# Order of weight roundings and PSUM banks in the two hybrid mixers of a two-block network

## Chip, cores and metric

The kernel runs on one core of a Trainium2 chip. The metric is the device time of one execution in microseconds, from the first to the last instruction of the core with what lies around it. The names of the engines in profile rows: PE is TensorE (PEld its weight loads), DVE is VectorE, ACT is ScalarE, POOL is GpSimd, SP is the engine that issues most of the DMAs.

## What is computed

The program is a whole network on a sequence of 512 tokens with 1024 features. The first block has two layers; each is half a feed-forward network, a hybrid mixer, and half a feed-forward network again. The second block (a bidirectional delta-rule mixer, experts) isn't touched. Of the reference, cut to the mixer:

```python
def first_block(x, ...):
    for l in range(2):
        x = x + 0.5 * swiglu_ffn(rms_norm(x, ffn1_norm_w[l]), ...)
        x = x + hybrid_mixer(rms_norm(x, mix_norm_w[l]), l, w_in[l], w_out[l], ...)
        x = x + 0.5 * swiglu_ffn(rms_norm(x, ffn2_norm_w[l]), ...)

def hybrid_mixer(h, ...):
    proj = h @ w_in
    mq, mk, mv, mo, mi, mf, z, xbc, dt_raw, dq, dk, dv = split(proj)
    # mLSTM of mq, mk, mv with the gates mi, mf; norm; times sigmoid(mo)
    xbc = silu(causal_dwconv(xbc, conv_w, conv_b))
    # state-space scan of xbc with dt_raw; times silu(z); norm
    # differential attention: two softmaxes of dq, dk with a bias,
    # first minus lam times second, times dv; norm
    return concatenate([y_mlstm, y_ssm, y_diff]) @ w_out
```

## The kernel before

Every engine has its own instruction stream, and each stage is a Python class that writes all of them. The class `Mixer` is the hybrid mixer; it is built twice, for layer 0 (it begins at about 434 us of the trace) and for layer 1 (at about 1634 us). `steps()` yields pairs (name, number), and `pe`, `act`, `dve` and `pool` walk over the same list of steps, each writing its own engine's share of a step. So the list sets the order on every engine, and a step that an engine has no share in costs it nothing.

**Weights.** Float32 precision comes from three products of rounded parts: a weight unit is 128x1024, and its high part (a cast to the rounded type on ScalarE, line 388) and its low part (weight minus high part, line 167) are made on the chip; `mm3` multiplies high by high, high by low and low by high. The step "split" j does both for unit j. The low part is made by VectorE for the mixer's units 0 to 3 and by GpSimd for all others (`lower`). There are three places for rounded units, so unit j may be cast only when the projection that read unit j-3 is done. `ahead(i)` yields "split" i+2.

**Projections.** `items` lists the mixer's 26 half blocks of `w_in`, numbered 0 to 25: xbc 0 to 7, mq and mk 8 to 11, mv 12 and 13, dq and dk 14 to 17, dv 18 and 19, z 20 to 23, mo 24 and 25, and then w_out. Item i reads unit i. The kind "fm" makes 128 output features for all tokens (24 products 128x512, a bank of its own for each of two in turn, `bank`). The kind "tok" makes 256 features for two token tiles at a time, and each of its two items needs both units of the pair: 12 products with the first unit, then 12 with the second, for each tile (`tok_pe`). The step "sum" i is item i on TensorE; "suma" i is the first half of an item (one token tile for "tok") which `steps` places before the left-over steps of the item before. Items 0 to 2 multiply the raw input (`raw_pe`), since the norm isn't there yet; VectorE multiplies their results by the norm's factor when it reads them (`raw_read`, within `scale_dve`, after inputs 1, 4 and 7). Item 3 and all later ones read the scaled input, of which `scale_dve` makes eight pieces (L177 and L167 in turn, with a cast on ScalarE, L494, between).

**Start of a mixer.** Steps: split 2, item 0, norm, split 3, item 1, scale, split 4, item 2 and so on. "norm" is on TensorE four sums over features, on VectorE mean and reciprocal (L173, L476), on TensorE the spread of the reciprocals (within item 1, behind its first two inputs), on ScalarE a table load and the square root. Item 2 waits until `there(0)`, VectorE's read of item 0, since both use bank 4. Behind item 5 TensorE transposes the small gate projections (line 157, 32x16); it waits for VectorE's copy L536, which stands in VectorE's order behind the convolutions of xbc.

**Attention.** "diff" n, n from 0 to 18, is a pipeline over 16 tiles (4 heads with 4 query tiles). On TensorE: the product with the values of tile n-3, the logits of tile n, the transposes of tile n-2. On ScalarE: a copy of the values' product (L2013), a copy of the transposes (L2018), and last the two exponentials of tile n (L182), which wait for VectorE. On VectorE: normalising tile n-1, adding scale and bias to the logits of tile n (L177, from PSUM), the maximum (L2052) and its negation (L172, 128x2). The steps of a projection are followed by those of `behind(i)`, of which `CUT` tells how many come before the next item's first half; for items 21 and 23 that is "diff" 3, "diff" 4 and "diff" 9, "diff" 10. For the second item of a "tok" pair, `ahead` follows the item's "sum": split 23 before "diff" 3, split 25 before "diff" 9.

Of the kernel before, what the change touches and what calls it, by code (L numbers as in the profile page):

```python
# [322 lines left out]
class Dense(Stage):  # L323
# [130 lines left out]
    def norm_pe(self, e, bank, n, there):  # L454

        self.norm_sum(e, bank, n, there)
        self.norm_spread(e, bank, n)
# [363 lines left out]
class Delta(Stage):  # L821
# [30 lines left out]
    def steps(self):  # L852
        for name in self.SETUP[4:] if self.ready else self.SETUP:
            yield name, 0
        for r in range(len(self.rounds)):
            for n in self.NAMES:
                yield n, r
                for x in self.after.during(r, n) if self.after else ():
                    yield ("then", *x), r
# [309 lines left out]
class Context(Conv):  # L1169
# [37 lines left out]
    def bank(self, i):  # L1207
        return self.k.bank[4 + i % 2]
# [324 lines left out]
class Mixer(Dense):  # L1533
# [125 lines left out]

    CUT = {6: 0, 7: 0, 13: 2, 14: 1, 15: 1, 16: 2, 17: 2, 18: 1, 21: 2, 22: 2, 23: 2, 24: 3}  # L1660

    def behind(self, i):

        if i == 0:
            yield "norm", 0
        elif i == 1:
            yield "scale", 0
        elif i == 3:
            yield "small", 0
        elif i == 4:  # L1670
            yield "ones", 0
        elif i == 5:
            yield "gates", 0
        elif i == 6:
            yield "cum", 0
        elif i == 7:
            yield "xs", 0
            yield "bias", 0
        elif i == 8:
            yield "silu", 7  # L1680
        for which, h in self.SSM.get(i, ()):
            yield "s" + which, h
        if i == 13:
            yield "crow", 0
        elif i == 14:
            yield "mt", 0
            yield "mA", 0
        if 16 <= i <= 19:
            yield "dsum", i - 16
        if 15 <= i <= 17:  # L1690
            yield "mA", i - 14
        if 15 <= i <= 18:
            yield "mB", i - 15
        if i == 19:
            yield "droot", 0
            for j in range(5):
                yield "mnorm", j
            yield "mroot", 0
        elif i == 20:
            for j in (0, 2, 1, 3):  # L1700
                yield "dfin", j
            yield "diff", 0
            yield "diff", 1
        elif 20 < i < 25:
            yield "diff", 3 * (i - 21) + 3
            if i == 24:
                yield "ssq", 1
            yield "diff", 3 * (i - 21) + 4
            yield "mnorm", i - 16
            if i == 24:  # L1710
                yield "sroot", 0
            yield "diff", 3 * (i - 21) + 5
        if i in (21, 23):
            yield "zgate", i // 2 - 10
        elif i == 22:
            yield "ssq", 0
        elif i == 24:
            yield "snorm", 0

    def steps(self):  # L1720
        yield "zero", 0
        yield from self.first()
        left = []
        for i in range(self.np):
            late = self.items[i].kind == "tok" and self.items[i].half
            if not late:
                yield from self.ahead(i)
            if left or i > 20:
                yield "suma", i
                yield from left  # L1730
                if i == 21:
                    yield "diff", 2
            yield "sum", i
            if late:
                yield from self.ahead(i)
            todo = list(self.behind(i))
            n = self.CUT.get(i, len(todo))
            yield from todo[:n]
            left = todo[n:]
        yield "diff", 15  # L1740
        yield "turn", 2
        yield "turn", 3
        yield "mo", 0
        yield "diff", 16
        yield "parts", 2
        yield "parts", 3
        yield "turn", 0
        yield "turn", 1
        yield "snorm", 1
        yield "diff", 17  # L1750
        yield "dnorm", 0
        yield "dnorm", 1
        yield "parts", 0
        yield "parts", 1
        yield "turn", 4
        yield "turn", 5
        yield "diff", 18
        yield "dnorm", 2
        yield "dnorm", 3
        yield "parts", 4  # L1760
        yield "parts", 5
        yield "part", 0
        yield "part", 1
        for t in range(5):
            yield "dnorm", 4 + t
        for c in (6, 7):
            yield "turn", c
            yield "parts", c
        for i in range(self.np, len(self.items)):
            yield from self.ahead(i)  # L1770
            yield "sum", i
# [14 lines left out]
    def bank(self, i):  # L1786

        if i >= self.np:
            return 4 + (i - self.np) % 4
        return 4 + self.nth(i) % 2  # L1790

    def nth(self, i):
        return sum(it.kind == "fm" for it in self.items[:i])
# [17 lines left out]
    def pe(self, e):  # L1811
        k, P, S, V, K, B = self.k, self.P, self.S, self.V, self.k.K, self.k.bank
        for name, i in self.steps():
# [7 lines left out]
                self.norm_spread(e, B[7], 512)  # L1821
                self.raw_pe(e, 1, range(2, 8))
            elif name == "sum" and i == 2:
                e.wait_ge(self.there(0))
                self.raw_pe(e, 2, range(8))
            elif name in ("sum", "suma") and i < self.np:
                it = self.items[i]
# [1687 lines left out]
```

## Time and profile before

| | |
|---|---|
| median of 3 runs | 3306.43 us (3302.94 to 3307.87) |
| the profiled execution | 3301.13 us, span 3299.3 us |
| PE busy | 3083.2 us (93%), x17336 |
| DVE busy | 1653.5 us (50%) |
| ACT busy | 1052.1 us (32%) |
| POOL busy | 217.6 us (7%) |
| granted TensorE clock, mean | 0.966 |

The profile is one execution. A busy share is an average over stages with different limits; what a change in a stage is worth is read from that stage's waits. In a timeline row the first number is the start, the second the duration, and the bracket at the end tells how long the engine stood idle before it and what released it.

### The profile page before, as it was taken

How to read it: one execution, taken by the hardware profiler on the slowest of the kernel's cores; microseconds unless marked ns; L12 is line 12 of the kernel's file. 1: busy time of each engine (PE TensorE's matmuls, PEld its weight loads, DVE VectorE, ACT ScalarE, POOL GpSimd, SP SyncE). 2: the span in 40 equal slices, each digit the busy share in tenths (PEclk: the TensorE clock that was granted, in tenths of full speed). 3: DMA queues.
4: the chain of work that ended last, by engine and by line, in shares of the span. 5: the costliest groups of instructions: out<-in, count | busy, mean ns of one | idle time of the engine just before them, and what ended most of it. 6: DMA issues, size and time to landing. Idle time of an engine off the chain costs nothing. (4 is left out here: it accounts for less than half of the span.)

```text
span 3299.3 us, 42166 instructions
## 1 busy us (share of the span) xinstructions
PE 3083.2 (93%) x17336; PEld 2349.0 (71%) x17336; DVE 1653.5 (50%) x3143; ACT 1052.1 (32%) x2148; POOL 217.6 (7%) x165
## 2 busy tenths in 40 slices
PE   8999999979999999999999889999898998887887
PEld 6777778768888878888778778888687887333333
DVE  5444485375555564555674564444644675211212
ACT  4222244353323243333344342222342553000002
POOL 0000012121000000000022220000001110000000
PEclk9999999989999999999999899999899889899999
DMA  4444421102223222122211112222211004999997
GB/s 187 185 163 150 150 84 61 42 27 96 96 77 124 81 96 93 68 71 83 90 52 52 39 52 92 92 92 90 86 64 64 2 2 195 366 420 421 421 421 328
DMA packets 66168, 443.39 MB, mean 134 GB/s; under 512 B 7476, under 2 KB 7732, under 8 KB 19640
## 3 DMA queue, kind: packets, MB, share of 16 engines
q1 hardware_dynamic: 61632, 425.75, 33.6%
q10 hardware_dynamic: 2648, 8.39, 0.7%
q0 software_dynamic: 1696, 6.55, 0.5%
q8 instruction: 137, 2.24, 0.3%
q14 instruction: 55, 0.45, 0.0%
HBM read 435.16 MB, written 5.51 MB: 134 GB/s over the span
## 5 line engine op out<-in xcount | busy, mean ns | idle before, releaser
L157 PE MATMUL ps<-b,b 128*128 128x512 f32 (+6 forms) x14038 | 2795.1, 391 | 153.1 <-DVE b L167 48.4
L157 PEld LDWEIGHTS ps<-b,b 128*128 128x128 f32 (+3 forms) x14038 | 2091.3, 183 | 821.7 <-issue 311.6
L167 DVE TENSOR_TENSOR b<-b,b 128x1024 fp32r<-128x1024 f32 (+7 forms) x743 | 611.8, 828 | 286.4 <-ACT b L388 167.0
L388 ACT CAST b<-b 128x1024 fp32r<-128x1024 f32 (+2 forms) x408 | 391.6, 961 | 419.8 <-PE ps L157 412.9
L167 DVE TENSOR_TENSOR b<-ps,b 128x64 f32<-128x64 f32 (+5 forms) x626 | 219.7, 366 | 299.3 <-PE ps L157 247.7
L157 PE MATMUL ps<-b 64*64 64x64 f32 (+10 forms) x2848 | 248.9, 276 | 31.2 <-ACT b L2018 17.4
L167 POOL TENSOR_TENSOR b<-b,b 128x1024 fp32r<-128x1024 f32 (+3 forms) x112 | 183.0, 1651 | 1368.1 <-ACT b L388 937.9
L157 PEld LDWEIGHTS ps<-b 64*64 64x64 f32 (+3 forms) x2848 | 211.6, 159 | 64.2 <-issue 20.2
L177 DVE SCALAR_TENSOR_TENSOR b<-ps,b 128x512 f32<-128x512 f32 (+3 forms) x272 | 142.4, 545 | 210.2 <-PE ps L157 184.6
L183 ACT ACTIVATE b<-b 128x512 f32<-128x512 f32 (+7 forms) x287 | 151.2, 533 | 210.8 <-DVE b L177 169.6
L167 DVE TENSOR_TENSOR b<-b,ps 128x512 f32<-128x512 f32 (+1 forms) x114 | 77.1, 678 | 279.5 <-PE ps L157 276.8
L177 DVE SCALAR_TENSOR_TENSOR b<-b,b,b 128x512 f32<-128x512 f32 (+3 forms) x224 | 170.4, 773 | 48.0 <-ACT b L183 43.7
L177 DVE SCALAR_TENSOR_TENSOR b<-ps,b,b 128x128 f32<-128x128 f32 (+3 forms) x164 | 83.5, 536 | 214.3 <-ACT b L183 116.7
L1479 ACT CAST b<-b 128x512 fp32r<-128x512 f32 x88 | 54.6, 621 | 412.7 <-DVE b L167 412.7
L183 ACT ACTIVATE b<-ps 128x512 f32<-128x512 f32 (+5 forms) x114 | 48.3, 437 | 338.7 <-PE ps L157 337.7
L177 DVE SCALAR_TENSOR_TENSOR b<-b,b 128x512 f32<-128x512 f32 (+6 forms) x235 | 135.0, 589 | 41.3 <-ACT b L183 39.0
L183 ACT ACTIVATE b<-b,b 128x128 f32<-128x128 f32 (+2 forms) x252 | 110.6, 477 | 140.4 <-DVE b L167 97.1
L183 ACT ACTIVATE b<-ps,b 128x128 f32<-128x128 f32 (+3 forms) x142 | 55.8, 432 | 122.9 <-PE ps L157 121.8
L286 PE MATMUL ps<-b,b 128*128 128x128 f32 (+1 forms) x450 | 73.5, 302 | 20.5 <-DVE b L177 9.4
L286 PEld LDWEIGHTS ps<-b,b 128*128 128x128 f32 (+1 forms) x450 | 54.6, 153 | 52.6 <-issue 25.0
L1044 ACT COPY b<-ps 128x128 f32<-128x128 f32 x240 | 60.2, 269 | 80.1 <-PE ps L157 71.0
L1159 POOL MEMSET b<- 128x128 f32 x12 | 2.5, 258 | 1005.0 <-DVE b L2695 581.5
(106 smaller groups left out, 569.0 us busy)
## 6 DMA issues: line engine op xcount, KB each, us to landing
b<-in_eg SPq DMA_DIRECT2D x64, 1024.0 KB, 27.4
b<-in_eu SPq DMA_DIRECT2D x64, 1024.0 KB, 27.2
b<-in_ed SPq DMA_DIRECT2D x64, 1024.0 KB, 26.9
b<-in_wg SPq DMA_DIRECT2D x44, 1024.0 KB, 4.8
b<-in_wu SPq DMA_DIRECT2D x44, 1024.0 KB, 4.8
b<-in_win SPq DMA_DIRECT2D x40, 1024.0 KB, 4.8
b<-in_wd SPq DMA_DIRECT2D x48, 768.0 KB, 4.1
b<-in_wmod SPq DMA_DIRECT2D x24, 1024.0 KB, 4.8
```

Of the source, the lines that this page charges most:

```text
L157: return e.h.matmul(out, l, r, start=start, stop=stop)
L167: return e.h.tensor_tensor(out, a, b, op)
L177: return e.h.scalar_tensor_tensor(out, a, s, b, op0, op1)
L183: return e.h.activation(out, a, f, bias=bias, scale=scale)
L286: return e.h.transpose(out, i, self.K["ident"][0:n, 0:n])
L388: e.h.copy(hi, src).then_inc(*self.S.tick(("hi", i)))
L1044: e.h.copy(self.LB[q][:, 0:128], B[:, 0:128]).then_inc(*S.tick((s, j, "L", lev + 1)))
L1159: z = e.h.memset(t, 0.0)
L1479: e.h.copy(self.ahi[:, f - self.f0[grp], :], t).then_inc(*S.tick(("ahi", f)))
```

## The change

In `behind(0)` the step "split" 3 is put ahead of "norm" (and left out ahead of item 1). Items 2 and 3 get the banks 0 and 1, which nobody else uses at that time; item 2's wait for `there(0)` goes, and with it, through `bank`, item 3's wait for the read of item 1, while items 4 and 5 wait for the reads of items 0 and 1 and not of 2 and 3. For items 21 and 23 the "split" moves behind the first step of `behind(i)` (`SPLIT`): "diff" 3, split 23, "diff" 4, and "diff" 9, split 25, "diff" 10. For the other second items of pairs the order stays.

```diff
--- before.py
+++ after.py
@@ -1659,9 +1659,12 @@
 
     CUT = {6: 0, 7: 0, 13: 2, 14: 1, 15: 1, 16: 2, 17: 2, 18: 1, 21: 2, 22: 2, 23: 2, 24: 3}
 
+    SPLIT = {21: 1, 23: 1}
+
     def behind(self, i):
 
         if i == 0:
+            yield from self.ahead(1)
             yield "norm", 0
         elif i == 1:
             yield "scale", 0
@@ -1723,7 +1726,7 @@
         left = []
         for i in range(self.np):
             late = self.items[i].kind == "tok" and self.items[i].half
-            if not late:
+            if not late and i != 1:
                 yield from self.ahead(i)
             if left or i > 20:
                 yield "suma", i
@@ -1731,10 +1734,11 @@
                 if i == 21:
                     yield "diff", 2
             yield "sum", i
-            if late:
-                yield from self.ahead(i)
             todo = list(self.behind(i))
             n = self.CUT.get(i, len(todo))
+            if late:
+                todo[self.SPLIT.get(i, 0):0] = self.ahead(i)
+                n += 1
             yield from todo[:n]
             left = todo[n:]
         yield "diff", 15
@@ -1787,7 +1791,7 @@
 
         if i >= self.np:
             return 4 + (i - self.np) % 4
-        return 4 + self.nth(i) % 2
+        return i - 2 if 2 <= i < 4 else 4 + self.nth(i) % 2
 
     def nth(self, i):
         return sum(it.kind == "fm" for it in self.items[:i])
@@ -1821,7 +1825,6 @@
                 self.norm_spread(e, B[7], 512)
                 self.raw_pe(e, 1, range(2, 8))
             elif name == "sum" and i == 2:
-                e.wait_ge(self.there(0))
                 self.raw_pe(e, 2, range(8))
             elif name in ("sum", "suma") and i < self.np:
                 it = self.items[i]
```

ScalarE at the start of the first mixer: the casts to b_125 and b_126 are the high parts of units 2 and 3; the table load, a one-element activation and the square root from PSUM (b_62) are the norm.

```order
 L183 ACTIVATE b_70<-b_60 128x512
 L388 CAST b_125<-b_53 128x1024
+L388 CAST b_126<-b_53 128x1024
 L183 ACT_TABLE_LOAD
 L183 ACTIVATE b_72<-b_72 128x1
 L183 ACTIVATE b_62<-ps 128x512
-L388 CAST b_126<-b_53 128x1024
 L494 CAST b_131<-b_69 128x512
 L494 CAST b_131<-b_70 128x512
```

The cast of unit 3 moved ahead of the norm, and the casts of the scaled inputs follow the square root directly.

VectorE at the same place: b_128 and b_129 are the low parts of units 2 and 3, b_71 the mean and its reciprocal, b_69 and b_70 the first scaled inputs.

```order
 L167 TENSOR_TENSOR b_128<-b_53,b_125 128x1024
+L167 TENSOR_TENSOR b_129<-b_53,b_126 128x1024
 L173 TENSOR_SCALAR b_71<-ps 128x4
 L476 RECIPROCAL b_71<-b_71 128x4
-L167 TENSOR_TENSOR b_129<-b_53,b_126 128x1024
 L177 SCALAR_TENSOR_TENSOR b_69<-b_60,b_56,b_62 128x512
 L177 SCALAR_TENSOR_TENSOR b_70<-b_60,b_56,b_62 128x512
```

The low part of unit 3 stands ahead of the mean and the reciprocal now, and no longer between them and the scaling.

ScalarE behind item 21 in the first mixer, before the change: L183 reads item 21's result, the cast to b_125 is unit 23, L2013 and L2018 are the copies of "diff" 3 and L182 its exponentials; the last two rows are the copies of "diff" 4.

```order
L183 ACTIVATE b_124<-ps 128x2x256
L388 CAST b_125<-b_51 128x1024
L2013 COPY b_124<-ps 128x64
L2018 COPY b_124<-ps 128x256
L182 ACTIVATE b_124,b_118<-b_124,b_118 128x512 x2
L2013 COPY b_124<-ps 128x64
L2018 COPY b_124<-ps 128x384
```

The same place with the change (the line numbers of the copies are three higher):

```order
L183 ACTIVATE b_124<-ps 128x2x256
L2016 COPY b_124<-ps 128x64
L2021 COPY b_124<-ps 128x256
L182 ACTIVATE b_124,b_118<-b_124,b_118 128x512 x2
L388 CAST b_125<-b_51 128x1024
L2016 COPY b_124<-ps 128x64
L2021 COPY b_124<-ps 128x384
```

The cast moved behind the exponentials of tile 3. Unit 25 moves in the same way behind the exponentials of tile 9, and both do so in the second mixer too.

## Rows read from the trace of the kernel before

**Rows 1.** Timeline, all engines, start of the first mixer (start us, us, engine, line; idle before).
```profile
435.61 1.05 ACT L388 CAST b<-b 128x1024 fp32r<-128x1024 f32 x1 [0.90 <-DVE b L167]
...
436.69 1.23 DVE L167 TENSOR_TENSOR b<-b,b 128x1024 fp32r<-128x1024 f32 x1 [0.96 <-ACT b L388]
...
438.02 0.18 DVE L476 RECIPROCAL b<-b 128x4 f32<-128x4 f32 x1
...
440.75 0.60 ACT L183 ACTIVATE b<-ps 128x512 f32<-128x512 f32 x1 [2.58 <-PE ps L157]
...
443.46 1.41 DVE L177 SCALAR_TENSOR_TENSOR b<-b,b,b 128x512 f32<-128x512 f32 x2
...
447.63 0.79 PE L157 MATMUL ps<-b,b 128*128 128x512 f32 x1 [2.72 <-DVE b L167]
```

**Rows 2.** Windows of TensorE: us, busy (count), granted clock, DMA share, GB/s.
```profile
447.50:451.00 3.50, 3.37 (x8) 0.51 0.03 12
```

**Rows 3.** Windows of all engines: PE, PEld, DVE, ACT, POOL busy, then clock.
```profile
441.60:485.50 43.90, 40.19 (x168) 30.78 (x167) 42.15 (x52) 15.54 (x22) 9.86 (x4) 0.92 0.20 72
```

**Rows 4.** Timeline of PE, first mixer, the join behind the sixth projection.
```profile
476.30 12.03 PE L157 MATMUL ps<-b,b 32*128 32x16 f32 x52 [0.99 <-DVE b L536]
```

**Rows 5.** Timeline of DVE, ACT and PE, the same places of the second mixer.
```profile
1638.62 0.18 DVE L476 RECIPROCAL b<-b 128x4 f32<-128x4 f32 x1
...
1642.76 1.41 DVE L177 SCALAR_TENSOR_TENSOR b<-b,b,b 128x512 f32<-128x512 f32 x2
...
1640.05 0.60 ACT L183 ACTIVATE b<-ps 128x512 f32<-128x512 f32 x1 [1.27 <-PE ps L157]
...
1646.93 26.13 PE L157 MATMUL ps<-b,b 128*128 128x512 f32 x112 [2.75 <-DVE b L167]
1675.61 14.62 PE L157 MATMUL ps<-b,b 32*128 32x16 f32 x62 [2.54 <-DVE b L536]
```

**Rows 6.** Timeline, all engines, attention tiles 3 to 5 of the first mixer.
```profile
652.59 1.03 ACT L388 CAST b<-b 128x1024 fp32r<-128x1024 f32 x1
...
653.69 2.36 POOL L167 TENSOR_TENSOR b<-b,b 128x1024 fp32r<-128x1024 f32 x1 [13.35 <-ACT b L388]
654.05 1.38 PE L157 MATMUL ps<-b 128*128 128x64 f32 x8 [2.51 <-ACT b L2018]
...
655.67 4.61 PE L157 MATMUL ps<-b,b 128*128 128x256 f32 x24
...
657.04 0.71 ACT L182 ACTIVATE b<-b,b 128x512 f32<-128x512 f32 x1
...
660.11 1.41 PE L157 MATMUL ps<-b 128*128 128x64 f32 x10
...
660.37 0.17 DVE L172 TENSOR_SCALAR b<-b 128x2 f32<-128x2 f32 x1
...
662.47 2.40 POOL L167 TENSOR_TENSOR b<-b,b 128x1024 fp32r<-128x1024 f32 x1 [6.41 <-ACT b L388]
662.47 0.75 DVE L177 SCALAR_TENSOR_TENSOR b<-ps,b 128x256 f32<-128x256 f32 x2
...
663.91 0.98 DVE L172 TENSOR_SCALAR b<-b 128x2 f32<-128x2 f32 x1
```

**Rows 7.** Timeline, all engines, attention tiles 9 and 10 of the first mixer.
```profile
685.96 0.17 DVE L172 TENSOR_SCALAR b<-b 128x2 f32<-128x2 f32 x1
...
687.00 0.51 ACT L182 ACTIVATE b<-b,b 128x256 f32<-128x256 f32 x1
...
687.16 3.55 PE L157 MATMUL ps<-b 128*128 128x64 f32 x12 [3.05 <-ACT b L2018]
...
690.74 1.02 DVE L177 SCALAR_TENSOR_TENSOR b<-ps,b 128x384 f32<-128x384 f32 x2 [0.87 <-PE ps L157]
```

**Rows 8.** Timeline of the second mixer, attention tile 9.
```profile
1884.97 0.17 DVE L172 TENSOR_SCALAR b<-b 128x2 f32<-128x2 f32 x1
...
1885.77 0.51 ACT L182 ACTIVATE b<-b,b 128x256 f32<-128x256 f32 x1
```

## Prediction

> **What bounds the kernel now.** TensorE is busy for 93% of the span, so I looked for the places where it stands still and asked what ended each wait. The change touches only the two mixers, and in each only three places: the start, attention tile 3 and attention tile 9. I read the timeline of all engines there, then windows for the granted clock, and left the rest of the program alone.
>
> At the start of the first mixer TensorE waits 2.72 us before projection 2, for the VectorE read of projection 0 that empties bank 4 [rows 1]. In the second mixer it is 2.75 us [rows 5]. Behind the first of these waits the granted clock was 0.51 for 3.50 us, the 1.2 GHz level [rows 2]; that costs about 1.7 us of TensorE work. But VectorE is the engine to watch: from the rounding of projection 3's weights onwards it is busy 42.15 of 43.90 us [rows 3], and TensorE then waits for it again before the small transposes, 0.99 us in the first mixer [rows 4] and 2.54 us in the second [rows 5]. So the start is a VectorE chain. Its head is: reciprocal of the norm, spread on TensorE, square root on ScalarE, the rounding of unit 3, and then the first scale at 443.46 [rows 1].
>
> In the attention part the chain goes back and forth between VectorE (logits, maximum, negation, L172) and ScalarE (exponentials, L182). TensorE waits 2.51 us for a copy on ScalarE that stands behind the cast of unit 23 [rows 6], and 3.05 us in the same way at tile 9 [rows 7].
>
> **The change, part by part.** Nothing is added or taken away on any engine; TensorE, GpSimd and the DMA queue keep their order. Three things move.
>
> *A. Start of a mixer.* Unit 3 is cast directly behind unit 2's cast, which ends at 436.66 [rows 1]. A cast lasts 1.03 to 1.05 us, so it is done at 437.7, before VectorE has finished unit 2's low part (436.69 + 1.23 = 437.9). VectorE then does unit 3's low part, 1.15 us of spacing (1.23 less the overlap of neighbours), ahead of mean and reciprocal. The reciprocal ends at 439.35 and not 438.20. Does the square root come 1.15 us later? In the second mixer reciprocal to square root is 1.25 us (1638.80 to 1640.05) [rows 5], so there the whole 1.15 is paid. In the first it is 2.55 us [rows 1]: TensorE was itself late by 1.3, so between 0 and 1.15 is paid, and I take 0.5, since the spread at the lower clock also needs longer than at the higher. The scale follows the square root directly now. First mixer: 441.35 + 0.5 = 441.9 with the hand-over, against 443.46, a gain of 1.5. Second: 1640.65 + 1.15 = 1641.85, against 1642.76, a gain of 0.9. Bounds: 1.0 to 2.0 and 0.3 to 0.9 (the low one if the longer wait for the reciprocal lowers the clock there as in [rows 2]).
>
> The banks: TensorE begins projection 2 without the 2.72 and 2.75 us waits, less the late spread, so 2.2 and 1.6 us sooner, and in the first mixer perhaps without the spell of [rows 2]. I cost this at nothing beyond VectorE's gain, because it ends at the same join: TensorE arrives at the small transposes sooner and waits longer there for VectorE, which has no gap to close [rows 3]. Projections 3 to 5 have their inputs in time, since VectorE's whole chain comes sooner too. **A: -2.4 us.**
>
> *B. Tile 3 (unit 23).* The cast moves from 652.59 behind tile 3's exponentials, and these wait for VectorE; the last ends at 657.75 [rows 6]. So the cast runs 657.75 to 658.8, and GpSimd's low part (start 0.07 behind the cast, 2.36 us long [rows 6]) ends at 661.2 and not 656.05. What wins: the copy before TensorE's 2.51 us wait comes 1.0 sooner. That buys nothing, as the next logits are not read before VectorE's own work is done. What loses: TensorE's next half projection, 24 products [rows 6], takes its last 12 from unit 23. It would reach them at about 656.2 (653.1 for the copy, 1.6 to the first product as now, 1.4 for 12) and must stand until 661.2. Then come 12 products of 256 columns (112 of 512 columns took 26.13 us [rows 5], 0.23 each, so half of that each: 1.4 us) and the block with tile 5's logits, 1.41 [rows 6]: 664.1 with a hand-over. VectorE now reads them at 662.47; it would be 1.7 late. Some of that is given back: tile 5's negation, 0.17 us elsewhere, lasts 0.98 to 664.89, when GpSimd's operation of 662.47 + 2.40 ends [rows 6]; being later it isn't held, so about 0.8 returns. Left: 0.9 us. With one spell at 1.2 GHz after so long a stand it is 1.7 more, 2.6 us. Waits of 2.5 us and more in these rows were followed by one (the 24 products behind the 2.51 us wait took 4.61), so I take 2.6 per mixer; without a spell it is 0.9, with two in a row 4.3. **B: +5.2 us.**
>
> The new low part also lies over tile 4's negation (660.37 [rows 6]), which then ends at 661.2, 0.8 late; this is covered by TensorE's delay above. The Trainium skill ("SBUF — State Buffer", "Who interferes with whom") says that GpSimd and such a VectorE instruction exclude each other for the whole instruction and that issue order decides; the trace agrees, the 0.98 us above end with GpSimd's operation. By that rule the negation could lose a whole GpSimd operation, up to 2.4 us and not 0.8, if it came just behind its start; the sum would be up to 3.2 us more over both mixers.
>
> *C. Tile 9 (unit 25).* The same move, but here the negation was ready at 686.13 and the exponential began only at 687.00 [rows 7], for cast and copies were ahead of it. Without the cast it begins at 686.2: 0.8 gained, and TensorE's logits of tile 10, for which VectorE waited 0.87 us, come sooner by as much. In the second mixer it is 1885.14 against 1885.77 [rows 8], 0.6. Unit 25 is needed later than it is ready here: its cast would follow the second exponential at about 687.2, its low part ends near 690.6, and the products that want it come around 691. Bounds: 0 (if they do wait) to 2.0 and 1.0 (if the shorter wait also avoids the slow spell in the 3.55 us block [rows 7]). **C: -1.4 us.**
>
> DMA: two loads of output weights start behind these low parts, 5.2 and 1.6 us later. They are cast only after the whole attention part, tens of us on: nothing.
>
> **Sum:** -2.4 + 5.2 - 1.4 = +1.4 us. The profiled execution would go from 3301.13 to 3302.5. It lies 5.3 us under the median of the runs, so I apply the difference to the median: 3307.8. A measurement of this kernel tells about 0.2%, 6.6 us, from no change; the forecast is therefore "no difference that can be seen".
>
> **The rivals.**
> 1. *TensorE, not VectorE, sets the start.* Then 2.2 + 1.6 us and the spell's 1.7 count, -5.5 for A; with B at 0.9 twice and C at -1.4 it is -5.1: 3301.3. For it: both bank waits are real and vanish. Against it: [rows 3] leave VectorE under 2 us of slack, and the waits of [rows 4, 5] name it.
> 2. *Late unit 23 costs two spells* (the slower side). TensorE stands almost 5 us in the middle of a half projection, longer than any wait in these rows. With two spells B is 4.3 twice; unit 25's products wait as well and eat C's gain. -2.4 + 8.6 = +6.2: 3312.6. It decides against the change from B over 1.9 us per mixer, and visibly from about 5. Against it: the spell in [rows 2] lasted 3.5 us and ended while TensorE worked on.
> 3. *The start brings nothing.* The change doesn't do there what it says: projection 3 waits for the scaled inputs instead of the bank, and the late reciprocal takes back what the missing cast gave. Then +5.2 - 1.4 = +3.8: 3310.2. Against it: TensorE is not what the chain waits for after the square root.
>
> **How the numbers follow.** Forecast 0.58, rival 1 0.15, rival 2 0.15, rival 3 0.12. The best ends of all parts give -2.9 + 1.8 - 3.0 = -4.1, the worst -1.3 + 8.6 + 0 = +7.3; runs of one kernel here lie up to 3.5 us from their median. The range 3301.5 to 3312.0 takes in the forecast, rival 3, nearly all of the better side and most of rival 2. Over 0.2% faster needs rival 1 with more than its price: 0.05. Over 0.2% slower is the upper part of rival 2: 0.10. The rest, 0.85, is no difference.
>
> **What would show each step.** A: no TensorE wait before projection 2, first scale 1.5 and 0.9 us sooner after the end of the stage before, and a longer wait before the small transposes (about 2 and 3 us). A shorter wait there makes A wrong. B: TensorE stands near 5 us inside the 24 products behind tile 4's logits, with GpSimd as releaser, and the logits of tile 5 come 1.7 to 3.4 us later, counted from tile 3. If the 24 products stay at 3 to 4.6 us without a wait, B is wrong. C: tile 9's exponential directly behind its negation. A whole time outside the range would mean that shifts of a few us change waits or the clock in stages that I left out.

## The result and the profile after

| | before | after |
|---|---|---|
| median | 3303.34 us (3299.1 to 3308.33, 20 runs) | 3309.2 us (3306.48 to 3314.19, 20 runs) |
| ratio, 95% interval | | 1.0019 (1.0012 to 1.0026) |
| profiled execution | 3301.13 us | 3314.19 us, the slowest of its 20 |
| span | 3299.3 us | 3312.3 us |
| mean granted clock | 0.966 | 0.963 |

The change costs about 6 us: a little less than the 0.2% that I called the bound of what can be told, while the interval reaches beyond it. The 20 runs of the kernel before have a median 3.1 us under that of the three runs from which I predicted. One execution of the kernel before, beside the third group of the experiments below, took 7656 us and is in no ratio.

The page of the changed kernel, the span and the busy times:

```profile
span 3312.3 us, 42162 instructions
...
PE 3094.4 (93%) x17336; PEld 2359.9 (71%) x17336; DVE 1652.9 (50%) x3143; ACT 1052.0 (32%) x2148; POOL 219.0 (7%) x165
```

The same instructions are there, but TensorE is busy for 11.2 us more and the span is 13.0 us longer. Work that is the same in number took longer, and the mean granted clock is 0.963 instead of 0.966. (The span's difference is twice that of the medians, since one profile is the slowest of its kernel and the other among the faster ones.) Measured between the same instructions (VectorE's first one of a mixer, a memset, and the reduction of its last norm), the two mixers took 592.2 us before and 601.2 after; everything outside them took 2707.1 and 2711.1, and between 2707.9 and 2711.7 in the profiles of all the experiments. So 9.0 of the 13.0 us are inside the mixers, and the other 4.0 are about what executions differ by anyway.

By stretches, both mixers together, the 9.0 us are: -3.2 from the start to the gate projections, +2.2 from there to attention tile 0, +7.7 from tile 3 to tile 6, +0.2 from tile 9 to tile 11, +1.6 behind the last tile, +0.5 elsewhere. The +2.2 lie in a stretch that the change doesn't touch: in the 28 mixers of all the profiles it took 158.8 to 163.6 us, 161.0 in the mean of the 16 with unit 3 split early and 160.5 in that of the 12 without. How much of a gain at the start is left at tile 0 can't be told against that.

**The start.** Timeline of the changed kernel, all engines, start of the first mixer (start us, duration, engine, line; the bracket is idle time and releaser), which answers to [rows 1]:

```profile
435.89 2.00 ACT L388 CAST b<-b 128x1024 fp32r<-128x1024 f32 x2 [0.90 <-DVE b L167]
...
436.97 2.36 DVE L167 TENSOR_TENSOR b<-b,b 128x1024 fp32r<-128x1024 f32 x2 [0.96 <-ACT b L388]
...
439.44 0.18 DVE L476 RECIPROCAL b<-b 128x4 f32<-128x4 f32 x1
...
440.87 0.60 ACT L183 ACTIVATE b<-ps 128x512 f32<-128x512 f32 x1 [1.46 <-PE ps L157]
...
441.50 1.42 DVE L177 SCALAR_TENSOR_TENSOR b<-b,b,b 128x512 f32<-128x512 f32 x2 [1.88 <-ACT b L183]
```

The two casts and the two low parts stand together now, and the first scale follows the square root directly: 441.50 instead of 443.46, in a mixer that begins 0.28 us later (unit 2's cast at 435.89, not 435.61). Counted from that cast the reciprocal is 1.1 us later, as foreseen, but the square root isn't later at all.

Timeline of PE in the changed kernel, the projections and the join, first mixer and then second, answering to [rows 1, 4, 5]:

```profile
439.67 31.17 PE L157 MATMUL ps<-b,b 128*128 128x128 f32 x138 [1.12 <-DVE b L476]
...
474.36 23.09 PE L157 MATMUL ps<-b,b 32*128 32x16 f32 x100 [3.52 <-DVE b L536]
...
1645.85 31.21 PE L157 MATMUL ps<-b,b 128*128 128x128 f32 x138 [1.14 <-DVE b L476]
1680.54 19.81 PE L157 MATMUL ps<-b,b 32*128 32x16 f32 x91 [3.48 <-DVE b L536]
```

The waits of 2.72 and 2.75 us before projection 2 are gone; the waits at the join grew from 0.99 and 2.54 us to 3.52 and 3.48. TensorE is early and VectorE sets the time of the join.

**Attention tiles 3 to 5.** Timeline of the changed kernel, all engines, answering to [rows 6]:

```profile
653.98 0.38 ACT L2021 COPY b<-ps 128x256 f32<-128x256 f32 x1
654.41 2.64 PE L157 MATMUL ps<-b 128*128 128x64 f32 x8 [1.57 <-ACT b L2021]
...
657.53 2.91 PE L157 MATMUL ps<-b,b 128*128 128x256 f32 x12
...
659.05 1.03 ACT L388 CAST b<-b 128x1024 fp32r<-128x1024 f32 x1
...
660.10 0.75 DVE L177 SCALAR_TENSOR_TENSOR b<-b,b 128x512 f32<-128x512 f32 x1
660.16 2.89 POOL L167 TENSOR_TENSOR b<-b,b 128x1024 fp32r<-128x1024 f32 x1 [20.07 <-ACT b L388]
...
661.67 1.41 DVE L172 TENSOR_SCALAR b<-b 128x2 f32<-128x2 f32 x1
...
663.10 2.93 PE L157 MATMUL ps<-b,b 128*128 128x256 f32 x12 [2.66 <-POOL b L167]
665.83 2.53 PE L157 MATMUL ps<-b 128*128 128x64 f32 x10
...
668.39 0.76 DVE L177 SCALAR_TENSOR_TENSOR b<-ps,b 128x256 f32<-128x256 f32 x2 [3.31 <-PE ps L157]
```

The 24 products are in two halves of 12, with a stand of 2.66 us between them that GpSimd's low part ends. Each half takes 2.9 us: the spell at 1.2 GHz began before them. Windows of TensorE in the changed kernel (window, us, busy, granted clock, DMA share, GB/s):

```profile
640.00:654.25 14.25, 12.18 (x149) 1.00 0.01 2
654.25:671.50 17.25, 14.30 (x60) 0.51 0.18 62
```

From 654.25, when the wait of 1.57 us for the copy was about to end, TensorE was granted 0.51, the 1.2 GHz level, for 17.25 us in a row, over work and waits alike. The spell at the same place in the kernel before cost the 24 products about 1.5 us (4.61 instead of the 3.07 that they take at 2.4 GHz in a run below) and was over by tile 5.

**Attention tile 9.** Timeline of the changed kernel, all engines, answering to [rows 7]:

```profile
691.10 0.17 DVE L172 TENSOR_SCALAR b<-b 128x2 f32<-128x2 f32 x1
691.31 0.51 ACT L182 ACTIVATE b<-b,b 128x256 f32<-128x256 f32 x1
...
694.44 1.02 DVE L177 SCALAR_TENSOR_TENSOR b<-ps,b 128x384 f32<-128x384 f32 x2 [0.74 <-PE ps L157]
```

The exponential follows its negation by 0.04 us instead of 0.87, as foreseen. From tile 9 to tile 11 it is nevertheless 11.6 us in both mixers, against 12.2 and 10.8 before.

### The profile page after: what moved, and what is told of

Same layout as the page of the kernel before. It is cut to its first block and busy times, and to the rows that moved or that the text cites. A ratio compares the mean times of both kernels' runs of the same rounds, so it can differ in the third digit from the quotient of the medians.

```text
span 3312.3 us, 42162 instructions
## 1 busy us (share of the span) xinstructions
PE 3094.4 (93%) x17336; PEld 2359.9 (71%) x17336; DVE 1652.9 (50%) x3143; ACT 1052.0 (32%) x2148; POOL 219.0 (7%) x165
## 5 line engine op out<-in xcount | busy, mean ns | idle before, releaser
L177 DVE SCALAR_TENSOR_TENSOR b<-ps,b 128x512 f32<-128x512 f32 (+3 forms) x272 | 142.5, 546 | 219.7 <-PE ps L157 194.1
L183 ACT ACTIVATE b<-b 128x512 f32<-128x512 f32 (+7 forms) x287 | 151.2, 533 | 218.8 <-DVE b L177 177.5
L177 DVE SCALAR_TENSOR_TENSOR b<-b,b,b 128x512 f32<-128x512 f32 (+3 forms) x224 | 170.3, 773 | 51.8 <-ACT b L183 47.5
L177 DVE SCALAR_TENSOR_TENSOR b<-ps,b,b 128x128 f32<-128x128 f32 (+3 forms) x164 | 83.6, 537 | 215.3 <-ACT b L183 116.9
L183 ACT ACTIVATE b<-ps 128x512 f32<-128x512 f32 (+5 forms) x114 | 48.2, 437 | 343.0 <-PE ps L157 341.9
L177 DVE SCALAR_TENSOR_TENSOR b<-b,b 128x512 f32<-128x512 f32 (+6 forms) x235 | 135.2, 589 | 41.2 <-ACT b L183 39.0
L183 ACT ACTIVATE b<-b,b 128x128 f32<-128x128 f32 (+2 forms) x252 | 110.6, 478 | 140.8 <-DVE b L167 97.6
L183 ACT ACTIVATE b<-ps,b 128x128 f32<-128x128 f32 (+3 forms) x142 | 55.7, 431 | 123.0 <-PE ps L157 122.0
```

The costliest lines, as they stand in the source:

```text
L177: return e.h.scalar_tensor_tensor(out, a, s, b, op0, op1)
L183: return e.h.activation(out, a, f, bias=bias, scale=scale)
```

## The experiments

Twelve kernels in three groups, each group with 27 to 33 runs of the kernel before on the same chip; their medians were 3302.77 us beside A, B, C and "A, cast between", 3303.86 beside A+B, the two halves of A and the changed kernel with idle products, and 3304.66 beside the rest. So medians of different groups aren't compared directly, the ratios are. I call the three parts A (start), B (tile 3, unit 23) and C (tile 9, unit 25) as above. The column "us" is the ratio's distance from 1 times 3303 us, with its 95% interval. The other columns are from one profile of each kernel. "3-6" is the time from the first maximum of attention tile 3 to that of tile 6, in each mixer; "end" is from the first maximum of tile 15 to the mixer's last norm; "mixers" is the sum of both mixers, measured as above.

| kernel | median us (n) | ratio | us | 3-6 | end | mixers |
|---|---|---|---|---|---|---|
| before | 3303.34 (20) | 1 | | 16.90, 16.90 | 13.07, 13.10 | 592.2 |
| changed (A+B+C) | 3309.20 (20) | 1.0019 | +6.3 (4.0 to 8.6) | 20.73, 20.73 | 13.07, 14.70 | 601.2 |
| A | 3301.87 (11) | 0.9995 | -1.7 (-4.6 to 1.3) | 16.90, 16.90 | 13.06, 13.14 | 590.5 |
| A, banks alone | 3305.18 (11) | 1.0000 | 0.0 (-3.0 to 3.0) | 16.90, 16.90 | 13.09, 13.06 | 595.5 |
| A, split alone | 3301.26 (11) | 0.9990 | -3.3 (-6.3 to -0.3) | 16.89, 16.90 | 13.07, 14.69 | 592.3 |
| B | 3312.64 (6) | 1.0031 | +10.2 (6.3 to 14.2) | 19.82, 19.54 | 13.07, 13.07 | 599.2 |
| A+B | 3309.51 (11) | 1.0016 | +5.3 (2.3 to 8.3) | 19.95, 19.86 | 13.06, 13.05 | 597.7 |
| B one tile later | 3317.36 (5) | 1.0038 | +12.6 (7.9 to 17.2) | 23.29, 23.18 | 13.07, 14.70 | 606.1 |
| A, cast between | 3301.25 (11) | 0.9995 | -1.7 (-4.6 to 1.0) | 17.06, 17.08 | 13.07, 13.06 | 591.2 |
| changed, idle products | 3305.66 (11) | 1.0006 | +2.0 (-1.0 to 5.0) | 18.42, 18.85 | 14.50, 14.70 | 593.6 |
| before, idle products | 3303.65 (11) | 0.9997 | -1.0 (-4.0 to 2.0) | 16.89, 16.90 | 13.06, 13.09 | 592.4 |
| C | 3305.79 (12) | 1.0010 | +3.3 (0.3 to 6.3) | 16.91, 16.89 | 14.70, 13.11 | 589.3 |
| A+C | 3308.03 (11) | 1.0004 | +1.3 (-2.0 to 4.3) | 16.90, 16.91 | 14.59, 14.56 | 594.3 |
| split alone, cast between | 3301.46 (11) | 0.9990 | -3.3 (-6.3 to -0.3) | 17.06, 17.07 | 13.05, 13.06 | 590.9 |

### Each part alone

The start alone (e1_start_only):

```diff
-    SPLIT = {21: 1, 23: 1}
+    SPLIT = {}
```

> Part A alone (unit 3's split early, banks 0 and 1; units 23 and 25 where they were before). Theory of the ledger: the gates' point of each mixer comes 2.2 us (first) and 0.9 us (second) sooner, counted from the mixer's start, as in the changed kernel, the attention tiles show no step, and the whole is 2 to 3 us faster than before. Rival, that the start costs more than it gives because TensorE's longer stand at the join (3.5 us) lowers its clock afterwards: the gain at the gates' point is gone by the first attention tile, and the whole is within 1 us of before or slower.

Tile 3 alone (e2_tile3_only); for tile 9 alone (e3_tile9_only) the table is `{23: 1}`, the rest the same:

```diff
-    SPLIT = {21: 1, 23: 1}
+    SPLIT = {21: 1}
...
         if i == 0:
-            yield from self.ahead(1)
             yield "norm", 0
...
-            if not late and i != 1:
+            if not late:
...
-        return i - 2 if 2 <= i < 4 else 4 + self.nth(i) % 2
+        return 4 + self.nth(i) % 2
...
             elif name == "sum" and i == 2:
+                e.wait_ge(self.there(0))
```

> Part B alone (cast of unit 23 behind tile 3's exponentials, all else as before). Theory: this is what the change loses; the maximum of tile 5 comes 4 to 5 us later counted from tile 4, 3.8 us of it are still there at tile 6, in both mixers, and the whole is 7 to 8 us slower than before. Prediction as recorded: 2.6 us per mixer, 5.2 in all. Rival, that the loss lies in stages outside: under 3 us.

> Part C alone (cast of unit 25 behind tile 9's exponentials). Recorded prediction: 1.4 us faster in all. From the changed kernel's trace: tile 10 comes 1.4 and 0.3 us sooner, tile 11 gives 0.8 back because TensorE waits for unit 25's low part, so between 1 us faster and 1 us slower in all.

A stands at -1.7 us, with an interval that takes in 0; B loses 10.2, C 3.3, each give or take 3 to 4. The three don't add up to +6.3 (-1.7 + 10.2 + 3.3 = 11.8). Beside A, B comes out at 7.0 and C at 3.0 (below), but the intervals are too wide to say that A makes B cheaper. B is the loss, and its place is the one foreseen: in its profile "3-6" is 2.9 and 2.6 us longer. That is 5.6 us; where the rest of the 10.2 lies, if it is real, that one profile doesn't show. Timeline of tile 3 alone, PE, GpSimd and VectorE around tile 5 of the first mixer:

```profile
652.33 0.66 PE L157 MATMUL ps<-b 128*128 128x64 f32 x4 [1.57 <-ACT b L2021]
...
661.03 2.93 PE L157 MATMUL ps<-b,b 128*128 128x256 f32 x12 [2.66 <-POOL b L167]
663.76 1.62 PE L157 MATMUL ps<-b 128*128 128x64 f32 x10
...
665.40 0.76 DVE L177 SCALAR_TENSOR_TENSOR b<-ps,b 128x256 f32<-128x256 f32 x2 [2.38 <-PE ps L157]
```

The wait of 2.66 us and the half rate of the 12 products behind it are the same as in the changed kernel. But the clock is back sooner: the block with tile 5's logits takes 1.62 us here and 2.53 there, and VectorE waits 2.38 us for it and not 3.31. That is why "3-6" is 19.5 to 20.0 us here and in A+B, and 20.73 in the changed kernel. A+B and the changed kernel have the same code up to tile 9; why the spell lasts longer in the latter isn't shown.

### What of A does it

Banks alone (e4_banks_only) and early split alone (e5_split_only), against the changed kernel:

```diff
 # banks alone
-    SPLIT = {21: 1, 23: 1}
+    SPLIT = {}
-            yield from self.ahead(1)
-            if not late and i != 1:
+            if not late:
 # early split alone
-    SPLIT = {21: 1, 23: 1}
+    SPLIT = {}
-        return i - 2 if 2 <= i < 4 else 4 + self.nth(i) % 2
+        return 4 + self.nth(i) % 2
+                e.wait_ge(self.there(0))
```

> Of part A only the banks: items 2 and 3 in banks 0 and 1, unit 3's split where it was. The prediction said that banks alone give nothing, as VectorE sets the join: the gates' point 44.8 us behind the mixer's start as without part A (43.9 with it), and the whole within 1 us of before. Rival, TensorE sets the start: the gates' point 1.5 us or more sooner.

> Of part A only the early split of unit 3; item 2 waits for bank 4 as before. Prediction: this is where VectorE's gain comes from, the gates' point 43.9 us behind the mixer's start in both mixers (44.8 without), 1.6 us faster than before in all. Rival: it needs the banks too and gives nothing alone.

I timed from the mixer's start to the end of the gate projections' chain. With the old order and banks it takes 44.81 to 44.85 us in all eight mixers of four kernels' profiles, and 46.12 and 44.82 in that of the kernel before; 44.81 in both mixers with the new banks alone; and with the early split 43.86 to 43.90 in 12 of 16 mixers, 44.1 to 44.4 in the rest, whatever the banks. At this point the early split is worth 0.93 us per mixer and the banks nothing. Timeline of PE with banks alone, first projections and join of the first mixer:

```profile
434.94 18.21 PE L157 MATMUL ps<-b,b 128*128 128x512 f32 x85 [1.15 <-DVE b L177]
...
474.90 23.43 PE L157 MATMUL ps<-b,b 32*128 32x16 f32 x100 [4.81 <-DVE b L536]
```

And with the early split alone:

```profile
475.02 12.07 PE L157 MATMUL ps<-b,b 32*128 32x16 f32 x52 [2.51 <-DVE b L536]
```

With banks alone TensorE stands 4.81 us at the join, against 2.54 in the second mixer before [rows 5]: most of what the bank waits took is waited here.

The predicted 1.5 us for the first mixer was read from one execution. That profile has 46.12 us where other executions of the same code have 44.82. Windows of TensorE in the profile before, the norm's stretch and the one behind it:

```profile
434.00:446.00 12.00, 9.88 (x43) 0.86 0.32 111
446.00:454.00 8.00, 6.37 (x21) 0.79 0.21 87
```

The same windows of the kernel before with idle products (below), whose start is the same code:

```profile
434.00:446.00 12.00, 8.57 (x44) 1.00 0.45 159
446.00:454.00 8.00, 7.58 (x26) 0.79 0.06 24
```

A spell such as that of [rows 2] is in both and costs the chain nothing: the second has it and takes 44.82 us. The 1.3 us go with an earlier one, over the norm's spread, that only the first of the two has. So the changed kernel is 2.2 us shorter to the gates than the profile before, and 0.9 us shorter than other executions of that same start.

### B: the wait or the clock

Start and tile 3 together (e10_start_tile3, the changed kernel with `SPLIT = {21: 1}`):

> Parts A and B (start and unit 23; unit 25 where it was before). If the parts add: A is -1.6 and B +9.9 us from the runs alone, so 8 us slower than before, 3311 us. If part C was part of the loss, this is faster than the changed kernel (3309.2 us); if C gave something back, slower. In the trace tile 5 comes 7 to 8 us behind tile 4 in both mixers, tiles 9 to 11 as in the kernel before.

A+B is 7.0 us above A, and the whole change 1.0 us above A+B. Two groups and an interval of some 3 us on each term leave that rough, but not the order: B is the big term.

The cast behind tile 4's exponentials instead of tile 3's (e14_later, otherwise as tile 3 alone):

```diff
-    SPLIT = {21: 1}
+    SPLIT = {21: 2}
```

> The cost of part B doubled: only unit 23's cast moved, and this time behind the exponentials of tile 4 instead of tile 3, 3.3 to 4.5 us later still. Theory (TensorE stands in the half projection until the low part is there, tile 5's logits stand behind it, and its clock falls): from tile 3 to tile 6 it takes 3 to 5 us more than with part B alone (19.5 to 20.7 us), so 23 to 25 us, and the whole 6 to 10 us more than with part B alone, 3319 us or more. Rival, that the cost of B is the longer wait of ScalarE or the clock alone and doesn't grow with the delay: within 2 us of part B alone (3312.6).

Timeline of this kernel, tile 5 of the first mixer:

```profile
661.31 4.67 POOL L167 TENSOR_TENSOR b<-b,b 128x1024 fp32r<-128x1024 f32 x2 [23.66 <-ACT b L388]
...
663.71 2.93 PE L157 MATMUL ps<-b,b 128*128 128x256 f32 x12 [6.03 <-POOL b L167]
...
668.51 0.76 DVE L177 SCALAR_TENSOR_TENSOR b<-ps,b 128x256 f32<-128x256 f32 x2 [7.12 <-PE ps L157]
```

The wait grows from 2.66 to 6.03 us and "3-6" by another 3.5 us per mixer. By the profile the price follows the lateness of unit 23 nearly us for us. The runs give a step from +10.2 to +12.6, with intervals of 4 to 5 us on each. It has the right sign but isn't clear of the noise, and the 3319 us or more that I expected were not reached.

The cast between the copies and the exponentials of tile 3 (e6_between, with A as in the change):

```diff
-    SPLIT = {21: 1, 23: 1}
+    SPLIT = {}
...
                 # diff_act, behind the copy of the transposes
+        if n == 3:
+            self.split_act(e, 23)
...
             elif name == "split":
-                self.split_act(e, i)
+                if i != 23:
+                    self.split_act(e, i)
```

> Part A, and the cast of unit 23 between the copies and the exponentials of tile 3 on ScalarE (unit 25 where it was before). ScalarE stands idle there for 3.3 us in both kernels, so the cast fits in without holding anything, and unit 23's low part is ready 0.5 us later than before instead of 7 us. Theory: no step at tile 5, TensorE's stand before the second tile's values 1 us shorter, the whole 2 to 4 us faster than before. Rival, that any low part of unit 23 that starts behind tile 3's logits costs: tile 5 comes 1 us or more later than in the kernel before.

Timeline of this kernel, all engines, tile 3 of the first mixer:

```profile
653.01 1.06 ACT L388 CAST b<-b 128x1024 fp32r<-128x1024 f32 x1
653.18 0.66 PE L157 MATMUL ps<-b 128*128 128x64 f32 x4 [1.57 <-ACT b L2021]
...
654.15 2.35 POOL L167 TENSOR_TENSOR b<-b,b 128x1024 fp32r<-128x1024 f32 x1 [13.73 <-ACT b L388]
...
655.80 4.55 PE L157 MATMUL ps<-b,b 128*128 128x256 f32 x24
...
656.56 0.72 ACT L182 ACTIVATE b<-b,b 128x512 f32<-128x512 f32 x1 [2.49 <-DVE b L172]
```

Here the copy is as early as in the change (1.57 us of wait and not 2.51), the cast lies in time in which ScalarE is idle (2.49 us are left before the exponential), and the 24 products run without a stop. B's cost is gone but for 0.2 us: "3-6" is 17.06. So the loss comes from the cast's place behind the exponentials, not from the earlier copy. It gains nothing either.

The changed kernel with idle products (e7_filler), whose results nobody reads, in the two stands:

```diff
                 # diff_pe, ahead of the wait for tile 1's values
+            if u == 1 and 6:
+                for _ in range(6):
+                    mm(e, B[4][:, :], self.hp(0)[0][:, 0:128], self.hp(0)[0])
...
             # tok_pe, ahead of the wait for unit 23's low part
+                if k == 4 and i == 22 and tiles == (0,) and self.name[:3] == "mix" and self.name != "mixb":
+                    for _ in range(16):
+                        mm(e, self.k.bank[4][:, :], src(0)[0][:, 0:128], src(0)[0])
```

> The changed kernel with 6 idle products (512 columns, into a bank that nobody reads) while TensorE waits for the copy before tile 1's values, and 16 more between the 12th and the 13th product of the half projection that waits for unit 23's low part. Together about 5 us at the full clock, within the stand of the changed kernel. Theory: the clock falls because TensorE stands, and the fallen clock makes tile 5 late by 4.6 us instead of 1.7. With the stands filled, no low clock from tile 3 to tile 5, tile 5 comes 5.0 us behind tile 4 (7.9 in the changed kernel, 3.3 in the one before), and the whole is 4 us or more faster than the changed kernel. Rival, that the clock isn't it and the late low part alone sets tile 5: 7.9 stays and the time stays at about 3309 us or rises.

Timeline of this kernel, tile 5 of the first mixer:

```profile
651.80 1.66 PE L157 MATMUL ps<-b,b 128*128 128x256 f32 x12
653.29 3.83 PE L157 MATMUL ps<-b 128*128 128x512 f32 x16
...
654.99 2.93 POOL L167 TENSOR_TENSOR b<-b,b 128x1024 fp32r<-128x1024 f32 x1 [18.52 <-ACT b L388]
...
657.97 1.68 PE L157 MATMUL ps<-b,b 128*128 128x256 f32 x12 [0.85 <-POOL b L167]
...
660.92 0.76 DVE L177 SCALAR_TENSOR_TENSOR b<-ps,b 128x256 f32<-128x256 f32 x2 [0.96 <-PE ps L157]
```

Window of TensorE in the same kernel:

```profile
648.00:666.00 18.00, 16.28 (x107) 1.00 0.17 59
```

The idle products hold 2.4 GHz over the whole window and the two halves take 1.7 us each instead of 2.9. VectorE waits 0.96 us for tile 5's logits instead of 3.31, and "3-6" falls from 20.73 to 18.42 and 18.85. That is 2.3 and 1.9 us of the 3.8 that B costs per mixer here. In the first mixer the rest, 1.5 us, is what the late low part costs at 2.4 GHz. The second mixer is no clean case: a spell stood over its first half (2.91 us), and the 16 idle products ended 0.5 us behind the low part. The whole kernel lies 4.3 us under the changed one by the ratios (+6.3 to +2.0, from two groups whose intervals overlap).

The same idle products in the kernel before (e9_filler_before), 8 in the stand of [rows 6]:

```diff
+            if u == 1 and 8:
+                for _ in range(8):
+                    mm(e, B[4][:, :], self.hp(0)[0][:, 0:128], self.hp(0)[0])
```

> Control for the idle products: the kernel before with 8 of them (1.9 us at the full clock) in TensorE's stand of 2.5 us before tile 1's values. Nothing waits there for TensorE, so by the theory tile 5 stays 3.3 us behind tile 4 and the whole within 1 us of before; the low clock that followed this stand is shorter or gone. If the clock as such carried the time, it would be 1.5 us or more faster; if idle products themselves delay, slower.

There they also remove the spell. Timeline of PE in this kernel, tile 4 of the first mixer:

```profile
655.84 3.07 PE L157 MATMUL ps<-b,b 128*128 128x256 f32 x24
```

The 24 products take 3.07 us and not 4.61, and "3-6" is 16.89 as before. At this place in the kernel before, a spell costs nothing, since VectorE and ScalarE set the pace; behind a late unit 23 VectorE waits for TensorE, and then the spell counts.

### C and the version that is left

Start and tile 9 together (e11_start_tile9, the changed kernel with `SPLIT = {23: 1}`):

> Parts A and C (start and unit 25; unit 23 where it was before). Recorded prediction for C -1.4 us, for A -2.4: 3.8 us faster. By the runs so far A is about -2 and C between 0 and +3: from 2 us faster to 1 us slower. In the trace: tile 9's exponential directly behind its negation, tiles 9 to 11 in 9.8 to 10.2 us against 10.6 to 12.6 without C, and, if C loses what it gains, a low clock in the turn of the outputs (from the maximum of tile 15 to the last norm 14.7 us instead of 13.1).

Timeline of PE in this kernel, unit 25's products and then the start of the output projection, first mixer:

```profile
691.18 1.09 PE L157 MATMUL ps<-b,b 128*128 128x256 f32 x7 [1.36 <-POOL b L167]
...
729.43 1.81 PE L157 MATMUL ps<-b 128*128 128x64 f32 x8
731.00 9.85 PE L157 MATMUL ps<-b,b 128*128 128x512 f32 x36
```

The same two last rows with the start alone:

```profile
729.13 1.00 PE L157 MATMUL ps<-b 128*128 128x64 f32 x8
729.94 8.61 PE L157 MATMUL ps<-b,b 128*128 128x512 f32 x36
```

Windows of TensorE, first with start and tile 9, then with the start alone:

```profile
723.50:733.70 10.20, 8.59 (x36) 0.50 0.15 64
```

```profile
723.50:733.70 10.20, 8.83 (x49) 0.83 0.20 84
```

Tiles 9 to 11 come closer together (9.79 us in both mixers, against 12.23 and 10.76 in the profile before and 10.2 to 12.9 in the other kernels without C), though unit 25's products wait 1.36 us for their low part. But "end" is 14.6 instead of 13.1: the lower clock stands over the first products of the output projection, which take 9.85 us and not 8.61. That is so in 6 of 8 mixers with C and in 2 of the 20 without it. In this window the granted clock is 0.50 with C and 0.83 without; why it stays low longer isn't shown. The runs give C no gain: +3.3 alone, 3.0 above A beside it, 1.0 above A+B. I can't say which of these is its price: the profile of C alone was of its fastest execution and shows the shortest mixers of all, while its 12 runs reach from 3299.57 to 3314.73 us, four times as wide as those of A. What the slower ones of them lose, and where, no profile here shows.

Early split, old banks, cast between (e12_split_between):

> What the runs point to: unit 3's split early (the part of A that gives), the banks as before, and unit 23's cast between the copies and the exponentials of tile 3. Theory: gates' point 43.9 us, no step at tile 5, 3 us faster than before (3301 us), as the early split alone. If the cast between adds something of its own, 1 us more.

3301.46 us, 0.9990 (0.9981 to 0.9999), the same as the early split alone. Both beat the kernel before by some 3 us and the changed one by 8 to 10. The cast in between adds nothing, as the 0.94 us that the copy comes sooner is waited elsewhere.

## Why the prediction came out as it did

The forecast time, 3307.8 us, is 1.4 us from the median, and "no difference that can be seen" holds at 1.0019. The difference was not well forecast: +1.4 against about +6. That the time fits better is luck: the median of three runs on which I put the sum was 3.1 us above that of 20. By difference, rival 2 (+6.2) is the nearest.

**A, right in mechanism, -2.4 predicted, -1.7 (-4.6 to 1.3) measured.** VectorE sets the start, the banks bring nothing, the waits at the join grew to 3.5 us where I had said 2 and 3. The measured interval takes in 0; the early split alone, at -3.3 (-6.3 to -0.3), is clear of it. The second mixer's 0.9 was exact (0.93). The first mixer's 1.5 was too much by 0.6 against the usual execution, though the changed kernel is 2.2 us shorter there than the profile that I read: I had taken the gap between reciprocal and square root there for TensorE's lateness by 1.3 us that every execution has, and it was a spell in the one that I read. Rival 1 is out, since the banks alone left the chain to the gates at 44.81 us, and rival 3, since the early split makes it 0.93 us shorter.

**B, the step that failed.** Predicted +2.6 per mixer, +5.2 in all; the runs say +7.0 beside A and +10.2 alone. In the profiles "3-6" is 2.6 to 3.1 us longer per mixer in B alone and A+B, near what I had, and 3.8 in the changed kernel itself. I had expected one spell, behind a stand of 5 us, over the last 12 products. What happened:
- TensorE stood 2.66 us there, not 5. The clock fell before, behind the 1.57 us wait for the copy, so that the first 12 products took 2.9 us and not 1.4 and filled part of the time.
- The spell didn't end with them. It went on for 17.25 us, over the last 12 products (2.93) and the block with tile 5's logits (2.53 where I had 1.41). Both were on the chain now.
- GpSimd's low part took 2.89 us, not 2.36: it began at 660.16 under a VectorE instruction that ran from 660.10 to 660.85 (see the last section).
- The return of 0.8 us behind the late logits came.

So two terms were mis-sized in the changed kernel. The late low part costs 1.5 us at 2.4 GHz and not 0.9, and the low clock costs 2.3 and not 1.7, since it lasted over the whole place; the sum is near my bound of two spells (3.8 measured, 4.3). In B alone and A+B the low clock cost 1.1 to 1.5. The error behind it: I counted a spell as a fixed price, read where other engines set the pace, and didn't ask what it costs where TensorE does. My reason for it was also misread: I wrote that the waits of 2.5 us and more in the rows were followed by a spell, but [rows 5] show one of 2.75 us that wasn't (112 products in 26.13 us). Filling the stands took away 1.9 to 2.3 us per mixer, about half of the loss.

The negation of tile 4 was held for 1.41 us (0.98 in [rows 6], 0.17 where GpSimd doesn't work), 1.2 us longer and so inside the 0.8 to 2.4 that I had; it ends at 663.08, GpSimd's operation at 663.05. This lies beneath TensorE's delay, as I had argued.

**C, the gain that wasn't kept.** The exponential behind its negation, as foreseen; unit 25's products wait up to 1.4 us with C alone and A+C, the case in which I had put the gain at 0. What I left out is what comes after: in 6 of 8 mixers with C the low clock stands over the 36 products of the output projection, which gives 1.4 to 1.6 us back. In the changed kernel tiles 9 to 11 brought nothing either, 11.6 us in both mixers against 12.2 and 10.9 in A+B. That moving work by a us moves the spells is my reading; no run tests it. Predicted -1.4; measured +3.3 alone, whose interval excludes a gain, and +1 to +3 beside the other parts, whose intervals don't.

## What to carry to other kernels

Before an operation is moved behind another engine's chain, write down when its last consumer wants it; ScalarE had 2.5 us of idle time two instructions earlier, in which the cast cost 0.2 us at most. Price a spell of lower clock by who sets the pace at that place: at one and the same place low clock cost nothing before the change, and filling the stands gave back up to 2.3 us per mixer after it. And read a stage in several executions or in its second copy in the program before a gain is taken from one; 0.6 of the 1.5 us predicted for A's first mixer were in one profile alone.

## What the runs showed of the hardware

- The granted clock fell to 1.2 GHz behind a wait of 1.57 us amid work (0.51 from 654.25), and not behind one of 2.75 us in the second mixer, where 112 products took 26.13 us [rows 5]. The length of a single wait doesn't tell it.
- It stayed low for 17.25 us, in which TensorE was busy for 14.30. Idle products in the stands kept it at 1.00 over the 18 us around the same place in the first mixer.
- Executions of the same code differ in where the spells stand: the start of the first mixer took 46.12 us in one profile and 44.82 in four others. The Trainium skill ("TensorE: Matmul & The Clock Gate", "What's actually happening") says of a kernel's beginning that the number of slow matmuls changes from run to run; here it is so in the middle of a program as well.
- GpSimd's low part of 128x1024 takes longer when it begins while VectorE is in the middle of an instruction whose row shows two or more inputs, all of them in SBUF (L177 or L173, b<-b,b or b<-b,b,b). In the mixers of all 14 profiles it took 2.52 to 2.55 us with 0.28 or 0.29 us of such an instruction left, 2.70 to 2.75 with 0.48 or 0.49, and 2.89 to 2.95 with 0.69. With nothing running on VectorE at its start (444 times), or with an instruction that reads PSUM (b<-ps,b, up to 0.61 us left), it took 2.34 to 2.43. The other way round, a VectorE instruction of 128x2 that began while it ran took 1.41 us instead of 0.17 and ended with it.
